# One step of a hybrid decoder layer: first loads in halves, an eighth gate pair as block products, and several small moves

## The reference

```python
z = x @ w_in            # eight parts of 512 columns, then four gates of 1024
a: causal conv of width 4 -> r, i = sigmoid(block-diagonal maps) -> h_t = a_t h_{t-1} + b_t -> y_a = h * gelu(a_gate)
b: b_val * sigmoid(b_gate) -> causal conv of width 31 -> LayerNorm -> silu
c: trailing means (2, 4, 8, 16) minus token -> a map per group -> scale
d: d_b * conv_w3(d_c * d_h)
merged = sum over n of sigmoid(gate_n) * (branch_n @ w_branch[n])
x = LN(alpha * x + merged @ w_out)
x = LN(alpha * x + (silu(x @ w_ff_gate) * (x @ w_ff_up)) @ w_ff_down)
```

## Time and profile before

| | us |
|---|---|
| median of 3 runs (lowest, highest) | 941.07 (940.93, 941.18) |
| profiled execution, its own time | 940.77 |
| its span | 939.0 |
| TensorE busy | 922.2 (98%) |
| VectorE busy | 704.4 (75%) |
| ScalarE busy | 415.4 (44%) |
| GpSimd busy | 325.8 (35%) |
| granted TensorE clock, mean | 0.996 |

### The profile page before, as it was taken

The page is one execution under the profiler, slowest core; times in us unless marked ns, Lnnn a source line. Parts: engine busy times, 40 slices in busy tenths (PEclk is TensorE's granted clock), DMA queues, the critical chain, the costliest instruction groups (busy, mean ns, idle before and its releaser), DMA issues.

```text
span 939.0 us, 18699 instructions
## 1 busy us (share of the span) xinstructions
PE 922.2 (98%) x7311; PEld 918.6 (98%) x7311; DVE 704.4 (75%) x1032; ACT 415.4 (44%) x659; POOL 325.8 (35%) x260
## 2 busy tenths in 40 slices
PE   8999999999999999999999999999999999999995
PEld 8999999999999999999999999999999999999995
DVE  2799999899896898777777699888887878321125
ACT  4422232326657423545444357555554557222222
POOL 5765665658634453000006443000000004443324
PEclk9999999999999999999999999999999999999998
DMA  8633233322445623332433320443334333422202
GB/s 239 189 91 90 77 98 90 89 68 84 138 147 187 195 70 112 113 99 72 121 101 112 86 74 26 122 122 91 89 91 119 102 89 102 146 85 84 80 1 96
DMA packets 169109, 98.30 MB, mean 105 GB/s; under 512 B 4906, under 2 KB 164946, under 8 KB 169057
## 3 DMA queue, kind: packets, MB, share of 16 engines
q1 hardware_dynamic: 166825, 96.66, 35.4%
q10 hardware_dynamic: 2232, 0.92, 0.4%
HBM read 89.94 MB, written 7.62 MB: 104 GB/s over the span
## 4 chain that ended last, share of the span: by engine, by line
PE 91%; DVE 5%; POOL 2%; issue 1%; ACT 1%; DMA 0%; POOLq 0%; DVEq 0%
PE main L1274 48%; PE main L1426 26%; PE aux L1426 4%; PE aux L1274 4%; PE main L1498 3%; PE main L1688 1%; PE aux L1260 1%; POOL x_lo L720 1%; PE main L1307 1%; PE aux L1498 1%; DVE merged L2150 1%; DVE main L2147 0%; POOL w_lo L634 0%; DVE aux L2182 0%; DVE merged L2195 0%
## 5 line engine op out<-in xcount | busy, mean ns | idle before, releaser
L634 POOL TENSOR_TENSOR w_lo<-raw,w_hi 128x1024 fp32r<-128x1024 f32 (+1 forms) x100 | 231.4, 2318 | 566.6 <-ACT w_hi L757 566.0
L757 ACT ACTIVATE w_hi<-raw 128x1024 fp32r<-128x1024 f32 x128 | 135.1, 1057 | 152.9 <-PE main L1274 118.6
L1274 PE MATMUL main<-x_hi,w_lo 128*128 128x272 f32 x784 | 162.5, 288 | 1.0 <-ACT sig L874 1.0
L1274 PE MATMUL main<-x_hi,w_hi 128*128 128x272 f32 x784 | 162.2, 288 | 0.0
L1274 PE MATMUL main<-x_lo,w_hi 128*128 128x272 f32 x784 | 161.7, 288 | 0.0
L1274 PEld LDWEIGHTS main<-x_hi,w_lo 128*128 128x128 f32 x784 | 123.2, 188 | 1.3 <-ACT sig L874 1.3
L1274 PEld LDWEIGHTS main<-x_lo,w_hi 128*128 128x128 f32 x784 | 123.1, 188 | 0.0
L1274 PEld LDWEIGHTS main<-x_hi,w_hi 128*128 128x128 f32 x784 | 122.4, 189 | 0.0
L1808 DVE SCALAR_TENSOR_TENSOR aux<-glu_pad,miscT,aux 128x512 f32<-128x512 f32 x112 | 75.2, 748 | 0.0
L2135 DVE SCALAR_TENSOR_TENSOR scr<-x_lo,main 128x544 f32<-128x544 f32 x6 | 4.3, 722 | 86.9 <-PE main L1274 86.9
L1274 PE MATMUL main<-y,w_hi 128*128 128x272 f32 x400 | 66.2, 287 | 0.0
(11 more groups left out here) (423 smaller groups left out, 2602.6 us busy)
## 6 DMA issues: line engine op xcount, KB each, us to landing
raw<-in_w_in SPq DMA_DIRECT2D x64, 512.0 KB, 4.2
raw<-in_w_ff_gate SPq DMA_DIRECT2D x22, 512.0 KB, 4.0
raw<-in_w_ff_up SPq DMA_DIRECT2D x22, 512.0 KB, 5.0
raw<-in_w_branch SPq DMA_DIRECT2D x32, 256.0 KB, 3.4
raw<-in_w_ff_down SPq DMA_DIRECT2D x16, 512.0 KB, 3.7
raw<-in_w_out SPq DMA_DIRECT2D x8, 512.0 KB, 3.6
raw<-in_w_ff_down SPq DMA_DIRECT2D x8, 384.0 KB, 3.3
kept_sums<-g_made_hi SPq DMA_DIRECT2D x4, 544.0 KB, 3.8
```

Of the source, the lines that this page charges most:

```text
L634: pool.tensor_tensor(w_lo[s][:, 0:n, :], raw[s][:, 0:n, :], w_hi[s][:, 0:n, :].bitcast(F32), ALU.subtract).then_inc(w_lo_ready, 1)
L757: act.activation(w_hi[s][:, :, :], raw[s][:, :, :], ACT.Copy).then_inc(w_hi_ready, 1)
L1274: mm = pe.matmul(ps[:, h, :], w[s][:, k, :], x[:, h * HALF:(h + 1) * HALF], start=(first and k == 0 and j == 0), stop=(last and k == n - 1 ...
```

## The change

- Start: x tile 0 is loaded first, then half the weights of unit 0, tile 1, the other half, tiles 2 and 3. ScalarE splits the first half, VectorE copies the upper part of the second, GpSimd makes both lower parts; VectorE makes unit 1's lower part. Eight of the 14 dummy transposes come before x_sample. Half of `first_unit` comes ahead of tile 2.
- ScalarE computes a Sigmoid of one column after the Exp. `lambda_parts` (input of the Exp) moves ahead of the loop over c.
- The last pair of the second branch's quarter (q = 1, i = 3) prepares a block step for the first pair of q = 2.
- In the recurrence, ScalarE copies the states, makes the upper part of the branch output (`keep_states`) and adds 1 for `decay_start` of blocks 2 and 3; the reciprocal of the next block comes ahead of `branch_low`.
- The last four lower parts of the second half of the normalised x are VectorE's; some sums of x and the first left lower part change places.
- Tail: the first step of `finish` becomes `weigh`, residual_last(1) comes ahead of one finish, and tile 0 is weighed in halves around `last_scale`.

```diff
-GATE_QUADS = 7
-U_QUAD = U_MIX + 36
+GATE_QUADS = 8
+U_QUAD = U_MIX + 32
...
-    return i + (4 * q - 9)
+    return i + (4 * q - 8)
...
     sp.dma_start(xs_tok[:, :], x_s).then_inc(x_landed[4], 16)
-    unit(0, 0, in_col(0, 0))
     for j in range(SEQ // P):
         sp.dma_start(x_tok[:, j, :], x_p[:, j, :]).then_inc(x_landed[j], 16)
+        if j < 2:
+            half = slice(j * (KD // 2), (j + 1) * (KD // 2))
+            sp.dma_start(raw[0][:, half, :], in_col(0, 0)[:, half, :])\
+              .then_inc((first_landed, raw_landed[0])[j], 16)
...
-    for k in range(36):
+    for k in range(32):
...
     for g in range(GATE_QUADS):
-        q, i, u = 2 + (g + 1) // 4, (g + 1) % 4, U_QUAD + 4 * g
+        q, i, u = 2 + g // 4, g % 4, U_QUAD + 4 * g
...
-    for u in range(RING):
+    first = slice(0, KD // 2)
+    pool.wait_ge(first_hi_ready, 1)
+    pool.tensor_tensor(w_lo[0][:, first, :], raw[0][:, first, :], w_hi[0][:, first, :].bitcast(F32),
+                       ALU.subtract).then_inc(first_lo_ready, 1)
+    rest = slice(KD // 2, KD)
+    pool.wait_ge(w_hi_ready, 1)
+    pool.tensor_tensor(w_lo[0][:, rest, :], raw[0][:, rest, :], w_hi[0][:, rest, :].bitcast(F32),
+                       ALU.subtract).then_inc(w_lo_ready, 1)
+    pool.wait_ge(w_lo_ready, 2)
+    for u in range(2, RING):
         lo(u, u, 8)
...
+    lo(U_QUAD, 0, 8)
...
-    for k in range(KD):
+    for k in range(KD // 2):
         x1_lo(1, k)
...
-    hi(0, 0)
+    act.wait_ge(first_landed, 16)
+    act.activation(w_hi[0][:, 0:KD // 2, :], raw[0][:, 0:KD // 2, :], ACT.Copy).then_inc(first_hi_ready, 1)
...
-        if h == 0:
-            hi(1, 1)
+    act.wait_ge(w_hi_ready, 1)
+    hi(1, 1)
     hi(2, 2)
...
+        if first:
+            gt_high(0, 2)
...
-    def pairs(q, i, tails=False, jobs=False):
+    def keep_states(c):
+
+        act.wait_ge(scan_done, c + 1)
+        act.activation(h_last[:, c, 0:1], S[3][:, SEQ - 1:SEQ], ACT.Copy)
+        act.activation(h_last[:, c, 1:1 + B],
+                       steps(S[3][:, SEQ:NT])[:, :, T - 1:T].rearrange("p b o -> p (b o)"),
+                       ACT.Copy).then_inc(h_kept, 1)
+        act.wait_ge(rec_ready, c + 1)
+        act.activation(Y_A[:, c, :], S[2][:, :], ACT.Copy).then_inc(ya_hi_ready, 1)
+
+    def pairs(q, i, tails=False, jobs=False, to_quads=False):
         u = i * 4 + (U_MIX + 16 * q)
+        if to_quads:
+            gate(u, 0, 0)
+            keep_states(i)
+            act.wait_ge(unit_done, u + 3)
+            act.activation(halves(sig[1][:, :]), slot(0), ACT.Sigmoid).then_inc(tile_out[0], 1)
+            for j in range(2):
+                gt_high(0, j)
+            act.wait_ge(gt3_ready, 1)
+            used(u + 1, 1)
+            hi(u + 2 + RING, 2)
+            used(u + 3, 3)
+            return
...
-        if q == 2:
-            for j in range(2):
-                gt_high(0, j)
-            act.wait_ge(gt3_ready, 1)
...
-        if q == 2:
-            gt_high(0, 2)
-            branch_high(0)
         gate(u + 2, 2, 1)
+        if q == 1 and isinstance(i, int):
+            act.wait_ge(sqrt_ready, 2)
+            act.activation(th[:, 2:KW, :], th[:, 2:KW, :], ACT.Identity, bias=1.0).then_inc(one_th_ready, 1)
+        if q == 1:
+            keep_states(i)
...
     act.wait_ge(lam_ready, 1)
     act.activation(spv[:, 1, :], spv[:, 0, :], ACT.Exp).then_inc(z_ready, 1)
+    act.activation(bn_rs[:, 1:2, 0:1], ones[:, 0:1], ACT.Sigmoid)
     pairs(0, 0, tails=True)
...
-    with act.Fori(1, KD // 2) as i:
+    with act.Fori(1, KD // 2 - 1) as i:
         pairs(1, i)
-    pairs(2, 0)
-    for i in range(1, KD // 2):
+    pairs(1, KD // 2 - 1, to_quads=True)
+    for i in range(KD // 2):
...
     sum_high(0, 0, 1)
     sum_high(0, 0, 2)
     x_sum_high(1)
-    x_sum_high(2)
     act.wait_ge(unit_done, U_FF + 1)
     act.activation(halves(S[0][:, :]), slot(0), ACT.Silu).then_inc(tile_out[0], 1)
     left_high(0, 0)
+    x_sum_high(2)
     x_sum_high(3)
     right_high(0, 0)
...
+    for _ in range(8):
+        pe.transpose(aux[:, 1, 0:P], ident[:, :], ident[:, :])
     pe.wait_ge(x_landed[4], 16)
     for k in range(KD):
         mm = pe.transpose(aux[:, 3, k * 32:k * 32 + 32], xs_tok[:, k * P:k * P + P],
                           ident[0:32, 0:32])
     mm.then_inc(turned, 1)
-    for _ in range(14):
+    for _ in range(6):
         pe.transpose(aux[:, 1, 0:P], ident[:, :], ident[:, :])
...
+            pe.wait_ge(*((first_lo_ready, 1) if k < KD // 2 else (w_lo_ready, 1)))
...
-    for j in range(3):
-        turn_x(j)
-    pe.wait_ge(w_lo_ready, 1)
+    turn_x(0)
+    turn_x(1)
     first_unit(0, range(0, KD // 2))
+    turn_x(2)
     turn_x(3)
     first_unit(0, range(KD // 2, KD))
...
+            pe.wait_ge(h_kept, KW)
...
-            pairs(q, 0, xs, branch_ready)
-            gate_quad(q, 1, xs, branch_ready)
-            with pe.Fori(2, KD // 2) as i:
+            gate_quad(q, 0, xs, branch_ready)
+            with pe.Fori(1, KD // 2) as i:
                 gate_quad(q, i, xs, branch_ready)
...
+    ve.wait_ge(raw_landed[0], 16)
+    ve.tensor_copy(w_hi[0][:, KD // 2:KD, :], raw[0][:, KD // 2:KD, :]).then_inc(w_hi_ready, 1)
...
+    ve.wait_ge(w_hi_ready, 2)
+    ve.wait_ge(w_lo_ready, 1)
+    ve.tensor_tensor(w_lo[1][:, :, :], raw[1][:, :, :], w_hi[1][:, :, :].bitcast(F32), ALU.subtract)\
+      .then_inc(w_lo_ready, 1)
...
+    lambda_parts()
     for c in range(KW):
...
-        if c == KW - 1:
-            lambda_parts()
...
-        ve.wait_ge(th_ready, c + 1)
-        after(link(ve.tensor_scalar(s_d[:, :], th[:, c, :], 1.0, None, ALU.add)))
-        after(link(ve.reciprocal(s_d[:, :], s_d[:, :])))
+        if isinstance(c, int):
+            ve.wait_ge(th_ready, c + 1)
+            after(link(ve.tensor_scalar(s_d[:, :], th[:, c, :], 1.0, None, ALU.add)))
+            after(link(ve.reciprocal(s_d[:, :], s_d[:, :])))
+        else:
+            ve.wait_ge(one_th_ready, 1)
+            after(link(ve.reciprocal(s_d[:, :], th[:, c, :])))
...
-        after(link(ve.tensor_tensor_scan(s_x[:, :], s_a[:, :], s_b[:, :], 0.0, ALU.mult, ALU.add)))
-        link(ve.tensor_copy(h_last[:, c, 0:1], s_x[:, SEQ - 1:SEQ]))
-        link(ve.tensor_copy(h_last[:, c, 1:1 + B],
-                            steps(s_x[:, SEQ:NT])[:, :, T - 1:T].rearrange("p b o -> p (b o)")))
-        after(link(ve.tensor_tensor(s_b[:, :], s_x[:, :], agate[:, c, :], ALU.mult)))
-        after(link(ve.tensor_scalar(Y_A[:, c, :], s_b[:, :], 1.0, None, ALU.mult)))
+        ve.tensor_tensor_scan(s_x[:, :], s_a[:, :], s_b[:, :], 0.0, ALU.mult, ALU.add).then_inc(scan_done, 1)
+        ve.wait_ge(scan_done, c + 1)
+        ve.tensor_tensor(s_b[:, :], s_x[:, :], agate[:, c, :], ALU.mult).then_inc(rec_ready, 1)
+
+    def branch_low(c):
+
+        s_b = S[2]
+        ve.wait_ge(h_kept, c + 1)
+        ve.wait_ge(ya_hi_ready, c + 1)
         ve.tensor_tensor(Y_A[:, c + KW, :], s_b[:, :], Y_A[:, c, :].bitcast(F32), ALU.subtract)\
             .then_inc(ya_ready, 1)
...
-        ve.wait_ge(gelu_ready, 1)
-        if isinstance(i, int):
-            ve.wait_ge(sqrt_ready, 1)
-        else:
-            ve.wait_ge(sqrt_ready, 2)
-            decay_start(i)
         decay_and_input(i)
         product(1, i, 0)
         recurrence(i)
+        decay_start(i + 1)
+        branch_low(i)
         product(1, i, 1)
 
+    ve.wait_ge(gelu_ready, 1)
+    ve.wait_ge(sqrt_ready, 1)
     second_quarter(0)
     ch.flush()
-    with ve.Fori(1, KD // 2) as i:
+    ve.wait_ge(sqrt_ready, 2)
+    with ve.Fori(1, KD // 2 - 1) as i:
         ch.enter(i - 1, 2 + PER_REC)
         second_quarter(i)
-    ch.leave(KD // 2 - 1)
-
+    ch.leave(KD // 2 - 2)
+
+    last_i = KD // 2 - 1
+    decay_and_input(last_i)
+    recurrence(last_i)
     gt_two(0, U_QUAD)
+    branch_low(last_i)
+    product(1, last_i, 0)
     gt_third(0)
     gt_fourth(0)
-    product(2, 0, 0)
     gt_low(0, 0)
     gt_low(0, 1)
-    ve.wait_ge(w_lo_ready, U_QUAD)
-    w_low(U_QUAD, 0, 8)
+    ve.wait_ge(w_lo_ready, U_QUAD + 1)
     w_low(U_QUAD + 1, 1, 8)
+    product(1, last_i, 1)
+    w_low(U_QUAD + 2, 2, KW)
     gt_low(0, 2)
-    branch_out(0)
-    w_low(U_QUAD + 2, 2, KW)
-    product(2, 0, 1)
-    for i in range(1, KD // 2):
+    for i in range(KD // 2):
         gate_quad(2, i)
...
     last_sum(0, 0)
-    ve.wait_ge(affine_ready, KD + KH)
+    ve.wait_ge(x1_lo_ready, KD + KD // 2)
+    for k in range(KD // 2, KD):
+        cols = slice(HALF, NT)
+        ve.wait_ge(x1_hi_ready, KD + k + 1)
+        ve.tensor_tensor(x_lo[:, k, cols], merged[:, k, cols], x_hi[:, k, cols].bitcast(F32),
+                         ALU.subtract).then_inc(x1_lo_ready, 1)
+    ve.wait_ge(affine_ready, 2 * KD)
     ve.wait_ge(x_sum_ready, 1)
     sum_x(1, x_sum[:, 0, :, :], a11, ALU.subtract)
     sum_x_low(0)
     sum_low(0, 0, 1)
-    ve.wait_ge(affine_ready, 2 * KD)
     ve.wait_ge(x_sum_ready, 2)
     sum_x(2, a12, x_sum[:, 1, :, :], ALU.subtract)
+    ff_product(0, slot(1))
```

(24 more changed lines are left out.)

4 lines of the change are left out of this document (added).

## The result

The changed kernel takes **946.26 us** (median of 5 runs, 944.52 to 946.44) against 941.07 before: a ratio of 1.005 (95% interval 1.0038 to 1.0062). It is slower by 5.2 us, where 3.5 us of gain were forecast; the range (935.5 to 939.4) missed it. The profiled execution after took 945.48, its span is 943.6; before they were 940.77 and 939.0.

The account below looks back on a forecast made before the run. TensorE, busy 98% of the span, was taken to bound the kernel; 0.55 + 1.05 + 0.6 + 1.2 + 0.05 = 3.45 us of gain gave 937.6 us, range 935.5 to 939.4.

Parts of the forecast that it names:

- part 2: Sigmoid table: loaded early, so TensorE's wait for the sigmoid of unit 32 goes; gain 1.05 us, bounds 0.7 and 1.2.
- The slower one: Rival: the last spilled sum is fetched late in the second quarter's last pair, TensorE waits 7.4 us; 944.1 us, chance 0.05.
- Part 1: First loads: the new order starts the first product at about 9.8 us; gain 0.55 us, bounds 0 and 1.3.
- Part 3: Eighth pair as block products: twelve fewer matmuls save 1.50 us, a new stall costs 0.9; net gain 0.6, bounds -0.2 and 1.5.
- Part 4: Late lower parts: four go to VectorE and TensorE's stalls go; gain 1.2 of 1.95 us, bounds 0.7 and 2.0.
- Part 5: Tail: residual_last(1) goes first, but the output transfers set the end; gain 0.05 us, bounds -0.2 and 0.4.
- the two new waits: TensorE's waits ahead of the seventh product: 0.9 us in the first block step, 0.75 in the first feed-forward step.

Follow-up runs that it names:

- f1: The changed kernel with VectorE's statistics put ahead of the first step of the third weight sum: 941.07 us.
- h2: The changed kernel with statistics first and the old tail, without the eight dummy transposes ahead of the first input: 939.94 us.
- h1: The changed kernel with statistics first, the old tail and five more identity transposes between those of x tiles 0 and 1: 938.46 us.
- g1: The changed kernel with statistics first and with the start and tail as in the kernel before: 938.59 us.
- e3: The kernel before with the sigmoid table part alone (one-column Sigmoid after the Exp, lambda_parts ahead of the filter loop): 945.32 us.

## Why the prediction was wrong

**Its frame.** "What the change moves beside a busy TensorE costs nothing as long as it stays ahead of it. So for each edit I ask when the next operand is due." I asked it only near each edit. Two edits, start and table, shift VectorE against GpSimd behind them, and I never looked through the kernel for places with little slack, such as the 0.57 us at the fifth side product, to be read from the trace of before by setting TensorE's start there (261.44) against the end of VectorE's reading (260.87). The step that failed is the search for who is late next in **part 2**: it names ScalarE's sigmoid of unit 36, which held, and not VectorE's softplus and what stands behind it. The runs showed there a wait of 3.18 us, 1.35 of slow matmuls behind it, and 5.2 us that come back when the statistics go first (f1). No rival let a VectorE instruction become longer than in the trace of before. The slower one put its mechanism at the last spilled sum, which was in time.

**Part 1** forecast +0.55 and it was -0.8 in the profile, -1.2 over the runs. The first product was to start at 9.8 and started at 10.60; tile 1 landed at 8.45, not 7.8, and the first twelve products took 2.24, start to start, instead of the 1.44 in my sum (1.52 before); I had the slow phase as a possible loss of 0.3. I let what the Trainium skill ("TensorE: Matmul & The Clock Gate", part 1) says, 1.2 GHz at first and 2.4 after sustained activity, outweigh the row in which transposes stayed slow to 10.4; with them, products were slow until 12.05, and h2 finds no gain from them. I took no account of the gap that opens between tiles 0 and 1; filling it makes all twelve products fast (h1).

**Part 2** forecast 1.05. The wait of 1.02 went, and the stretch gained 1.28, just over my bound of 1.2: unit 34 now starts 0.03 behind the start of the last transpose instead of 1.30, of which I counted little more than the wait. Over the runs about 0.5 is left, but that is a difference of differences: the three profile terms, 2.5 together, match the 2.5 by which g1 lies below before. As a single edit it costs 4.4 us (e3).

**Part 3** forecast 0.6: the new wait was to be 0.9 and is 0.8, at the product forecast. This is TensorE's row, behind VectorE's third addition:

```profile
384.66 0.36 PE L1470 MATMUL main<-x_hi,gt_lo 128*128 128x272 f32 x1 [0.80 <-DVE sig L2132]
```

The step gained 0.44 in the profile, and the part 0.95 over the runs, within the bounds.

**Part 4** forecast 1.2: the stalls went (2.16 by the milestones at 580 us, 1.95 forecast), and 1.36 came back as waits behind VectorE's chain, 0.75 forecast. Net 0.80, or 0.93 over the runs. The count of VectorE's chain was right: its addition ended at 595.50, 4.08 later than before where the stage came in 4.50 later, so at 591.0 on the clock of before (591.1 forecast). But the seventh product, where I put the wait, doesn't wait for it. The mis-sized term is the 0.75: TensorE stops earlier in the step, by 0.40, 0.60 and 0.21 ahead of its third, fifth and sixth products (585.93, 589.62, 591.33), each behind a copy with which ScalarE empties a bank. The first two copies stand in ScalarE's queue behind sums that VectorE makes later than before, a path that I didn't look at.

**Part 5** forecast 0.05, with bounds of -0.2 and 0.4, and it is -0.9 in the profile and -1.2 over the runs. The step that failed is "GpSimd's three tiles run back to back and nothing of theirs moves": the last tile waits for ScalarE's rows, these for the scale, and the scale met GpSimd's own addition.

The three parts in which I added up VectorE's and ScalarE's queues near the edit came out at 2.5 in the profile against 2.85 forecast. The closeness is in part luck: one gained more than its bound, two gained less, and one of the two new waits stood elsewhere. What they gained was less than what an unexamined place, 0.57 us from its edge, cost.

## What to carry to other kernels

Before forecasting an edit that shifts engines against each other, list for the whole kernel how long before TensorE's use each operand is ready, smallest first, with the queues of ScalarE and of transfer issues in it; where a place has under a microsecond, put what TensorE waits for ahead of what nobody wants yet. Allow a chain of tiny VectorE operations up to one GpSimd instruction each where GpSimd is busy, not 0.17 us each (here eight or ten of fifteen were held, 10.7 or 15.0 us in all). And a stall of TensorE costs more than its length: price the slow matmuls behind it as well.
